# Layer norm tiles kept in the products' PSUM banks, and transposes, low parts and one projection moved earlier, in a six-stage transformer kernel

## What is computed

```python
x = _layernorm(DEEPNORM_ALPHA * x + y, ln_g[i], ln_b[i])      # y = branch(x), i = 0..3
# _layernorm: mu = mean(x); var = mean((x - mu)^2); (x - mu) * rsqrt(var + 1e-5) * g + b
```

## Time and profile before

| | |
|---|---|
| median of 3 executions | 1862.21 us (1861.24 to 1862.46) |
| the profiled execution | 1861.74 us, of which its span is 1859.9 us |
| granted TensorE clock, mean | 0.995 of full speed |
| PE, DVE, ACT, POOL busy | 97%, 50%, 40%, 33% of the span |
| traffic with device memory | 144.74 MB read, 2.10 MB written, 79 GB/s |

### The profile page before, as it was taken

How to read it: one execution, slowest core, us unless ns; L and a number is a source line. 1 busy time by engine, 2 the same in 40 slices (tenths; PEclk the granted TensorE clock), 3 DMA queues, 4 the chain that set the end, 5 groups by cost and what they waited for, 6 DMA issues and landing times.

```text
span 1859.9 us, 24990 instructions
## 1 busy us (share of the span) xinstructions
PE 1812.7 (97%) x10060; PEld 1448.7 (78%) x10060; DVE 927.9 (50%) x1976; ACT 747.7 (40%) x1617; POOL 622.8 (33%) x296
## 2 busy tenths in 40 slices
PE   7999999999999999999999999999999999999997
PEld 5787876688888888889766888887877777886666
DVE  4557766554211101144767366666534243576664
ACT  5333455453321222343545344553334233345452
POOL 4333421144444453443212333333332323322122
PEclk9999999999999999999999999999999999999999
DMA  5322311043333332324212232223331312322211
GB/s 177 96 68 69 91 51 31 23 148 110 117 91 102 95 110 84 97 79 102 49 36 80 80 94 69 69 69 85 88 78 57 79 58 86 97 55 47 52 56 68
DMA packets 215171, 148.45 MB, mean 80 GB/s; under 512 B 51968, under 2 KB 197392, under 8 KB 215056
## 3 DMA queue, kind: packets, MB, share of 16 engines
q1 hardware_dynamic: 210160, 135.27, 26.0%
q10 hardware_dynamic: 4896, 11.60, 1.7%
HBM read 144.74 MB, written 2.10 MB: 79 GB/s over the span
## 4 chain that ended last, share of the span: by engine, by line
PE 87%; DVE 9%; ACT 2%; issue 1%; DMA 0%; POOL 0%; ACTq 0%; DVEq 0%
PE PS L392 23%; PE PS L394 22%; PE PS L393 22%; PE PS L538 7%; PE PS L484 6%; PE PS L568 4%; DVE X L1460 1%; ACT sq L1027 1%; PE PS L542 1%; PE PS L703 1%; DVE X L1474 1%; DVE XTl L1468 1%; PE PS L918 1%; PE PS L897 1%; PE PS L724 0%
## 5 line engine op out<-in xcount | busy, mean ns | idle before, releaser
L2029 POOL TENSOR_TENSOR Wl<-Wr,Wh 128x1024 fp32r<-128x1024 f32 (+5 forms) x292 | 622.6, 2145 | 1202.9 <-ACT Wh L974 1202.5
L392 PE MATMUL PS<-XTl,Wh 128*128 128x512 f32 (+1 forms) x1096 | 413.4, 377 | 11.0 <-DVE XTl L1468 9.5
L394 PE MATMUL PS<-XTh,Wh 128*128 128x512 f32 (+1 forms) x1096 | 408.9, 373 | 0.0
L393 PE MATMUL PS<-XTh,Wl 128*128 128x512 f32 (+1 forms) x1096 | 408.7, 373 | 0.0
L974 ACT CAST Wh<-Wr 128x1024 fp32r<-128x1024 f32 (+5 forms) x292 | 267.7, 937 | 177.3 <-PE PS L394 139.6
L392 PEld LDWEIGHTS PS<-XTl,Wh 128*128 128x128 f32 x1096 | 207.2, 189 | 55.1 <-issue 12.7
L394 PEld LDWEIGHTS PS<-XTh,Wh 128*128 128x128 f32 x1096 | 207.2, 189 | 36.5
L393 PEld LDWEIGHTS PS<-XTh,Wl 128*128 128x128 f32 x1096 | 207.2, 189 | 34.6
L392 PE MATMUL PS<-Wl,XTh 128*128 128x512 f32 (+2 forms) x608 | 228.7, 376 | 2.7 <-DVE XTl L1468 1.8
L393 PE MATMUL PS<-Wh,XTl 128*128 128x512 f32 (+2 forms) x608 | 225.1, 370 | 0.0
L394 PE MATMUL PS<-Wh,XTh 128*128 128x512 f32 (+2 forms) x608 | 225.1, 370 | 0.0
(11 more groups left out here) (317 smaller groups left out, 2463.9 us busy)
## 6 DMA issues: line engine op xcount, KB each, us to landing
Wr<-in_w_in SPq DMA_DIRECT2D x38, 512.0 KB, 3.7
Wr<-in_fox_w_in SPq DMA_DIRECT2D x32, 512.0 KB, 4.1
Wr<-in_w_ffn_gate SPq DMA_DIRECT2D x22, 512.0 KB, 3.9
Wr<-in_w_ffn_up SPq DMA_DIRECT2D x22, 512.0 KB, 3.8
Wr<-in_w_ffn_down SPq DMA_DIRECT2D x22, 512.0 KB, 3.6
Wr<-in_swa_w_in SPq DMA_DIRECT2D x20, 512.0 KB, 3.9
Wr<-in_mla_w_in SPq DMA_DIRECT2D x16, 512.0 KB, 4.1
Wr<-in_mla_w_out SPq DMA_DIRECT2D x16, 512.0 KB, 3.5
```

The costliest lines, as they stand in the source:

```text
L392: pe.matmul(o, l[0], r[1], start=start, stop=False)
L393: pe.matmul(o, l[1], r[0], start=False, stop=False)
L394: return pe.matmul(o, l[0], r[0], start=False, stop=stop)
L2029: raw.tensor_tensor(l[:, 0:m], r[:, 0:m], h[:, 0:m].bitcast(F), sub).then_inc(*weight_lo.next(i))
```

## The change

It has five parts. (1) The layers' residual, centred and scaled values stay in the y bank: `residual` writes into it, ACT squares from it (its unused output goes to X), DVE centres in place, one half behind each square, and only the last operation writes X. The SBUF buffers XC and sq are gone, and a y bank of a layer is given free by "normed" instead of "y". (2) The Newton step is three `tensor_scalar` operations instead of four (three of them `tensor_tensor`), and the sum of the two halves' squares is a `tensor_scalar` instead of a `tensor_tensor`; both in all norms of `norm_tail` and in the first one. (3) For tiles 1 and 2, ACT's high and DVE's low part of the transposed tile i - 1 come ahead of tile i's squares and statistics instead of behind its scaling (in mix and ffn behind the first square on ACT). (4) Tile 3's transposes come ahead of the last product (piece) of pass 0, except in the mixer's first product. (5) In mla, `prep(0)` is moved ahead of the QRn transposes on PE and of the QRT copies on ACT and DVE, and g5 ahead of score 1; in fox, q2 is moved ahead of score 1 and `select(0)` ahead of v0's copies.

```diff
-            lambda p: [[("prep", 0), ("need", "g4")], [("prep", 1)]][p] if p < 2 else [], lambda p: [("need", f"v{p // 4}")],
+            lambda p: [[("need", "g4")], [("prep", 1), ("need", "g5")]][p] if p < 2 else [], lambda p: [("need", f"v{p // 4}")],
...
-        fox_steps = paced_steps(8, fox_jobs + ["g6", "g7"], [5, 3, 3, 4, 3, 3, 0, 1, 1], lambda p: [("need", f"q{p}"), ("need", f"k{p}")],
+        fox_steps = paced_steps(8, fox_jobs + ["g6", "g7"], [5, 3, 3, 4, 3, 3, 0, 1, 1], lambda p: [("need", f"q{p}"), ("need", f"k{p}")] + [("need", "q2")] * (p == 1),
...
                     c = slice(256 * h, 256 * h + 256)
-                    if h:
-                        turn_tile(before[s], 3)
                     for f, (((i, n, kts), b), (key, _, _)) in enumerate(zip(ws, products)):
-                        if h == 0 and f == 1:
-                            turn_tile(before[s], 2)
+                        if h == 0 and f in (1, len(ws) - 1):
+                            turn_tile(before[s], 2 if f == 1 else 3)
                         e.wait_ge(weight_lo.at(i), *free(b), normed(before[s], 2 * h + 1))
...
                             turn_tile(before[s], 2)
+                        elif h == 0 and f == len(ws) - 1:
+                            turn_tile(before[s], 3)
...
+                        give(bs[i][c], (by_dve, ("y" if s in ("ffn0", "ffn1", *rms) else "normed", s, i, c)))
...
+                prep(0)
...
                     after(psum_full, "y", s, i, 1)
+                    turns = s != "mla1"
                     if s in ("mix", "ffn"):
-                        for c in range(2):
-                            square(s, i, c, by_dve.at("y", s, i, c))
+                        square(s, i, 0, by_dve.at("y", s, i, 0))
+                    if turns and i in (1, 2):
+                        turned_tile(s, i - 1)
+                    if s in ("mix", "ffn"):
+                        square(s, i, 1, by_dve.at("y", s, i, 1))
                         rsqrt((s, i), st[:, 1:2], st[:, 3:4], st[:, 2:3])
                     else:
                         e.wait_ge(by_dve.at("mean", s, i))
                         for c in range(2):
-                            act.activation(XC[s][1][:, HALVES[c]], X[:, i, HALVES[c]], ACT.Square, bias=st[:, 2:3], accum_out=st[:, 4 + c:5 + c]).then_inc(
+                            act.activation(X[:, i, HALVES[c]], bank["y", s, i, c][:, :], ACT.Square, bias=st[:, 2:3], accum_out=st[:, 4 + c:5 + c]).then_inc(
                                 *by_act.next("square", s, i, c))
                         rsqrt((s, i), st[:, 14:15], st[:, 16:17], st[:, 15:16])
-                    if i and s != "mla1":
+                    if turns and i == 3:
                         turned_tile(s, i - 1)
 
...
 
+            def newton(key, dst, q, v):
+
+                e.wait_ge(by_act.at("rsqrt", *key))
+                ve.tensor_scalar(q, dst, dst, v, mult, mult).then_inc(*by_dve.next())
+                e.wait_ge(by_dve.now())
+                ve.tensor_scalar(q, q, -0.5, 1.5, mult, add).then_inc(*by_dve.next())
+                e.wait_ge(by_dve.now())
+                ve.tensor_scalar(dst, q, dst, None, mult).then_inc(*by_dve.next())
+                e.wait_ge(by_dve.now())
...
                 H = rms[s]
+                if s != "n0" and i in (1, 2):
+                    turned_tile(s, i - 1)
                 e.wait_ge(by_act.at("square", s, i, 1))
-                ve.tensor_tensor(st[:, 0:1], st[:, 4:5], st[:, 5:6], add).then_inc(*by_dve.next())
+                ve.tensor_scalar(st[:, 0:1], st[:, 4:5], st[:, 5:6], None, add).then_inc(*by_dve.next())
                 e.wait_ge(by_dve.now())
                 variance((s, i), st[:, 2:3], st[:, 0:1], 1.0 / D, 1e-6)
-                refined((s, i), st[:, 1:2], st[:, 3:4], st[:, 2:3])
...
-                st, x, xc = ST[:, i, :], X[:, i, :], XC[s][0]
+                st, x = ST[:, i, :], X[:, i, :]
                 ve.tensor_scalar(st[:, 2:3], st[:, 0:1], st[:, 1:2], -1.0 / D, add, mult).then_inc(*by_dve.next("mean", s, i))
-                e.wait_ge(by_dve.now(), gain_in[0].at(s), gain_in[1].at(s))
-                for cs in HALVES:
-                    ve.scalar_tensor_tensor(xc[:, cs], x[:, cs], st[:, 2:3], GB[:, 0, cs], add, mult).then_inc(*by_dve.next())
-                e.wait_ge(by_act.at("square", s, i, 1))
-                ve.tensor_tensor(st[:, 13:14], st[:, 4:5], st[:, 5:6], add).then_inc(*by_dve.next())
+                if s != "mla1" and i in (1, 2):
+                    turned_tile(s, i - 1)
+                e.wait_ge(by_dve.at("mean", s, i), gain_in[0].at(s), gain_in[1].at(s))
+                for c, cs in enumerate(HALVES):
+                    y = bank["y", s, i, c]
+                    e.wait_ge(by_act.at("square", s, i, c))
+                    ve.scalar_tensor_tensor(y[:, :], y[:, :], st[:, 2:3], GB[:, 0, cs], add, mult).then_inc(*by_dve.next())
+                ve.tensor_scalar(st[:, 13:14], st[:, 4:5], st[:, 5:6], None, add).then_inc(*by_dve.next())
                 e.wait_ge(by_dve.now())
                 variance((s, i), st[:, 15:16], st[:, 13:14], 1.0 / D, 1e-5)
-                refined((s, i), st[:, 14:15], st[:, 16:17], st[:, 15:16])
+                newton((s, i), st[:, 14:15], st[:, 16:17], st[:, 15:16])
                 for c, cs in enumerate(HALVES):
-                    ve.scalar_tensor_tensor(x[:, cs], xc[:, cs], st[:, 14:15], GB[:, 1, cs], mult, add).then_inc(
+                    ve.scalar_tensor_tensor(x[:, cs], bank["y", s, i, c][:, :], st[:, 14:15], GB[:, 1, cs], mult, add).then_inc(
                         *by_dve.next("normed", s, i, c))
 
...
-                ve.scalar_tensor_tensor(X[:, i, cs], X[:, i, cs], alpha, bank["y", s, i, c][:, :], mult, add,
-                                        accum_out=ST[:, i, c:c + 1] if s in XC else None).then_inc(*by_dve.next("y", s, i, c))
+                y = bank["y", s, i, c][:, :]
+                if alpha == ALPHA:
+                    ve.scalar_tensor_tensor(y, X[:, i, cs], alpha, y, mult, add, accum_out=ST[:, i, c:c + 1]).then_inc(
+                        *by_dve.next("y", s, i, c))
+                else:
+                    ve.scalar_tensor_tensor(X[:, i, cs], X[:, i, cs], alpha, y, mult, add).then_inc(*by_dve.next("y", s, i, c))
...
+                    if i == 3 and s != "mla1":
                         turned_tile(s, i - 1)
...
+            select(0)
             fox_job("v0")
             for kind, x in fox_steps:
                 if kind == "job":
                     fox_job(x)
                 elif kind == "score":
-                    if x == 0:
-                        select(0)
```

More of the change, by code:

```diff
@@ L288, in program @@
             f_att = attention(cm)
-            f_XC = centred(cm)
-        XC = {"mla0": m_XC, "swa": s_XC, "fox": f_XC, "mla1": m_XC}
         GT = {"mla0": m_GT, "swa": s_GT, "fox": f_GT, "mla1": m_GT}
@@ L438, in first_N @@
                 for h in range(2):
-                    if h:
+                    if h and s == "mix":
                         turn_tile(before[s], 3)
@@ L820, in job, with prep @@
                         proj_N((s, "v", c), [(w_kv[:, a, 8 * c:8 * c + 8, 64:128], 1) for a in range(2)], 512, CK, lambda t: c_ready, by_dve)
+                def prep(x):
+                    hs = (2 * x, 2 * x + 1)
+                    proj_T((s, "pq", x), [(w_q[:, :, h, 0:64], 64 * j) for j, h in enumerate(hs)], CQ, c_ready, (by_act, (s, "pq", x)))
+                    proj_T((s, "pk", x), [(w_kv[:, :, h, 0:64], 64 * j) for j, h in enumerate(hs)], CK, c_ready, (by_dve, (s, "pk", x)))
                 for f in range(3):
@@ L1306, in mla, with prep @@
                     act.mul(QRn[:, i, :], bank[s, "qr", i][:, :], scale).then_inc(*by_act.next(s, "qr", i))
+                def prep(x):
+                    after(psum_full, s, "pq", x)
+                    if x:
+                        after(scores_full, s, x - 1, 1, 3)
+                    act.mul(m_QT[:, :], bank[s, "pq", x][:, :], scale).then_inc(*by_act.next(s, "pq", x))
                 job("v0")
                 job("g3")
+                prep(0)
                 for c in range(4):
@@ L1316, in mla @@
                     elif kind == "prep":
-                        after(psum_full, s, "pq", x)
-                        if x:
-                            after(scores_full, s, x - 1, 1, 3)
-                        act.mul(m_QT[:, :], bank[s, "pq", x][:, :], scale).then_inc(*by_act.next(s, "pq", x))
+                        prep(x)
                     elif kind == "score":
@@ L1855, in mla, with prep @@
                     rope(x1, x2, x1, x2, cs[0], cs[1], RT[:, 0], RT[:, 1], s, "qn", i)
+                def prep(x):
+                    e.wait_ge(psum_full.at(s, "pk", x))
+                    if x:
+                        e.wait_ge(scores_full.at(s, x - 1, 1, 3))
+                    copy(m_KT[:, :], bank[s, "pk", x][:, :], s, "pk", x)
                 job("v0")
                 job("g3")
```

(6 more changed lines are left out.)

10 lines of the change are left out of this document (2 added, 8 removed).

## The result

The changed kernel takes 1845.93 us (median of 4 runs, 1845.27 to 1848.36) beside 1862.34 of the kernel before (4 runs, 1861.24 to 1862.67): a ratio of 0.9915, 95% interval 0.9898 to 0.9932, 16.4 us. Timed once more beside the experiments it took 1845.79 us (1844.97 to 1846.36), ratio 0.9913 (0.9900 to 0.9925). The first profiled execution took 1848.36 us, the slowest of its four, with a span of 1846.6, the second 1844.97 with 1843.1; before it was 1859.9.

A forecast was written before the change was run, and what follows sets the result against it. PE, busy 97% of the span, was taken as the bound. Gains 10.2 + 5.9 - 1.2 = 14.9 us, less 0.5 by choice, gave 1847.3 profiled, 1848 median; own range 1845 to 1851.5, with rivals 1844.5 to 1856.

The forecast's parts named there:

- Low parts: Layer boundaries: PE's waits on low parts fall from 11.4 to about 1 us; the boundary gains together give 10.2 us.
- the walk: Step-by-step timing of the swa to fox boundary, from PE's tile 0 transposes: pass 1 starts 27.65 -> 24.5, 3.15 us less.
- only PE's idle time can change: Whole kernel: matmuls are moved and none added, so PE's waits, 18.7 us, are all the change could take from PE.
- Part 1, contention: Tile 3's centring and scaling beside POOL: with a bank operand they run undisturbed, and tile 3 loses 3.9 us.
- net +0.3 us a tile: Layer-norm tile: centring now waits for squares, 0.6 us, partly recovered; net between -0.1 and +0.6.
- 686 against 748: DVE's ns per operation with a bank operand against SBUF, taken to return 0.12 us for the scaling pair.
- Rival C: DVE in layer norms: a bank costs 0.06 us more than SBUF, not less; 6.4 us lost, 1854; 8%.
- The rule beside it: Skill page's fixed VectorE cost, 120 cycles from PSUM, 58 from SBUF, estimated 65 ns more; the sum went by measured rows.
- The end: mla1's norm, ending the program: four tiles at +0.3 each cost +1.2 us, between -0.4 and +2.4.
- Part 5: Inside the stages: waits for QRn, at score 1 and for MB go, 2.0 + 2.6 + 1.5 - 0.2 = 5.9 us.
- rivals A and B: A: a tile's chain still outlasts PE, 1854, 14%. B: stage waits return behind the moved work, 1854, 8%.

The follow-up runs named there:

- experiment 2: Changed kernel with tile 3's transposes put back between pass 0 and pass 1: 1850.48 us, 4.7 above it.
- experiment 3: Changed kernel with high and low parts of tile i - 1 back behind tile i's scaling for tiles 1 and 2: 1857.37 us, 11.6 above it.
- experiment 1: Changed kernel with the moves inside the mla and fox stages undone: 1853.38 us, 7.6 above it.
- experiment 4: Changed kernel with residual, centring and scaling back in SBUF buffers instead of the y bank: 1853.50 us, 7.7 above it.
- experiment 7: Changed kernel with the old SBUF scheme in tiles 0 to 2 and the last norm, banks only in tile 3 of the other layer norms: 1846.29 us.
- Experiment 8's second kernel: Changed kernel with the SBUF scheme in tile 0 of each layer norm and all of the last norm: 1840.64 us, the fastest of all.
- experiment 9: Changed kernel without the y-bank scheme, plus 13 identity transposes ahead of each of PE's two waits for tile 3 of swa and of fox: 1849.76 us.
- experiment 6: Changed kernel with half 1 centred into X while half 0 is squared, in tiles 0 to 2 and the last norm: 1850.67 us, 4.9 above it.

## Why the prediction was right, and where it was wrong

The time (1848 for the median, 1847.3 for the profiled execution) stands beside 1845.9 and 1848.4, inside the forecast's own range. The mechanism held: the low parts' waits, the contention with POOL and the waits inside the stages went as described. But that the sum came so close is in part luck. The tile's price was over twice what I took, which cost 1.9 us at the end alone, and swa and mla1 gave some 0.6 us each less than forecast; against that stand 0.9 more in mla0 and 0.7 more in fox, where 1.4 us are PE's clock, which I had not priced at all. Point by point:

- **Low parts** (10.2 us of the sum). The waits went as walked, 11.4 to 0.2. At fox the walk said tile 3's transposes at 20.15 plus a wait of 0.2 to 0.5, and pass 1 at 24.5; it was 21.0 with 0.58 in it, and 25.0. Counted from the norm's start pass 1 came 2.1 us earlier (32.9 to 30.8), not 3.15 - 0.3: each tile was later than the +0.3 allowed. Experiments 2 and 3 show both moves at work, and that in mla1 part 4 loses 0.7.
- **Fox came out right for a reason I had not seen.** 2.1 us at the boundary and 2.5 from part 5 (experiment 1) make 4.6, and the trace has 6.2. Behind the wait of 1.81 us ahead of pass 1 the kernel before ran some 3.2 us of matmuls at the lower clock. Its timeline of PE, and stretches of it:

```profile
1302.15 0.28 PE L394 MATMUL PS<-XTh,Wh 128*128 128x256 f32 x1
1302.27 0.28 PE L392 MATMUL PS<-XTl,Wh 128*128 128x256 f32 x1
...
1302.99 0.41 PE L393 MATMUL PS<-XTh,Wl 128*128 128x256 f32 x1
1303.20 0.41 PE L394 MATMUL PS<-XTh,Wh 128*128 128x256 f32 x1
```

```profile
1303.00:1304.00 1.00, 1.00 (x6) 0.50 1.03 366
1304.00:1305.00 1.00, 1.00 (x7) 0.50 1.05 310
```

  A matmul started every 0.12 us at 1.00 and every 0.21 at 0.50, which is 1.2 GHz. 15 such steps from 1302.56 to 1305.76 cost 15 x 0.09 = 1.4 us, and 4.6 + 1.4 = 6.0. My reading took the waits' length for their whole price; "only PE's idle time can change" left out PE's clock.
- **Part 1, contention.** Right: 1.42 and 1.41 us beside POOL, the predicted 3.9 us of tile 3's own operations. But I counted it as the difference between two traces, whereas without the banks the other moves would have brought tile 2 into POOL's window as well (experiments 4 and 7). The Trainium skill's rule on who shares a port (page "SBUF — State Buffer", section "Who interferes with whom": a VectorE operation with at most one SBUF input, outside the two-port modes, does not contend with GpSimd) agrees with the rows shown here, and the one-column `tensor_scalar` took 0.2 us beside POOL, as I took from the row.
- **Part 1, "net +0.3 us a tile": the step that failed.** It was +0.78, beyond the +0.6 I gave as the bound. The second half of the centring, put at 0.6, stands 0.75 us between the last square and the sum. I let 0.12 us come back for "686 against 748", but the 686 belong to the residual, a different operation without the gain; in a bank the centring takes 754 and the scaling 747, and nothing came back. ACT's squares gave 0.08, about the 0.1 I took. The two residuals with their reads, put at nothing, take 0.09 more (a read of the sum takes 0.14 us instead of 0.08), and part 2 costs 0.03 instead of giving 0.07. 0.75 - 0.08 + 0.09 + 0.03 = 0.79. Rival C's condition did not hold, though the end cost 3.1 us as if it had.
- **The rule beside it.** The Trainium skill, page "VectorE: DVE Perf Modes", section on the TRN2 errata, has a VectorE operation from a bank 62 cycles dearer than one from SBUF. For these forms the traces show neither that nor what I had read in its place: 754 and 747 ns against 748 to 750.
- **The end**, 1.2 us predicted, 3.1 measured: four times the same error. Experiment 8's second kernel takes it back whole.
- **Part 5**, 5.9 us predicted, 6.8 shown by undoing it. No wait at score 0 or at turn 0 (rivals A and B).
- **mla0**, 1.9 predicted, 2.8 measured: 2.1 are part 5's. Part 2 is worth 1.4 there with the rest in place, where I had let ffn's tile 3 gain nothing on the path. The two do not add up to 2.8, since each is measured with the other in place.
- **The parts do not add up.** Undone one at a time they are worth 8.7 (part 1), 1.2, 11.2, 5.0 and 6.8 us of trace, 33 in all, for 14 together. Some 9 of the 33 are the lower clock behind the waits that came back (4.3 with part 1 undone, an estimated 4.5 with part 3). Parts 1 and 2 without the others are a loss of 8.9 us. Part 3's low pair fills the very wait that part 1 opens, and part 1 takes away the contention into which parts 3 and 4 bring tiles 2 and 3.

Left open: the 0.6 us between swa's two profiles, which differ by a wait for GT of 0.4; and mla1's part 4, where the fastest kernel with tile 3's transposes between the passes should be 0.7 us faster still by experiment 2. It was not run.

## What to carry to other kernels

A wait that an in-place buffer adds is free only where other work is there to fill it: in this kernel the bank paid where a low pair covers the squares or where POOL works, and the SBUF copy where the engine has nothing else to do (the first tile, the last norm). Compare durations of the *same* operation when you price a move between memories. And look at the granted clock behind each of PE's longer waits before you price it: here 1.4 to 2.2 us of slow matmuls stood behind waits of 1.8 to 4.3. Undoing one part of a change can show that part's worth only with the others in place.

## What the runs showed of the hardware

- **A wait of PE can cost the lower clock behind it.** The granted clock was 0.50, which is 1.2 GHz, for 3.4 us behind a wait of 1.81 in the kernel before, for 3.4 us at each of 3.25, 3.26 and 1.81 in experiment 3, and for 6.9 us at each pair of 2.1 to 2.2 in experiment 4. In all of these it fell while PE stood or within 1 us behind. With PE kept at work in those pairs it stayed at 1.00 and 3.7 us came back (experiment 9).
- **The wait's length alone does not tell whether it falls.** It stayed at 1.00 behind 2.33 and 2.29 us in the kernel before, behind 2.66 and 2.77 in experiment 7 and behind 2.76 in experiment 6, though it fell behind 2.25 there. Nor is it certain at a given wait: at the 2.94 us at 160 us it fell for 6.9 us in the profiles of the kernel before and of the changed one (granted 0.66 over 160 to 170 us) and not in the changed kernel's second (1.00), which makes the 2.8 us between their first norms. What decides was not settled.
- **Contention is paid on both sides.** Beside a pair of two-SBUF-operand operations POOL's pair took 5.59 us instead of 4.77, and DVE's 3.56 instead of 1.41 (experiment 7). With the operand in a bank neither lost anything.
- **A read of the accumulated sum** on DVE takes about 83 ns behind an operation that writes SBUF and 141 behind one that writes a bank (medians of 32 in the kernel before and in the changed one).
